# A two-block transformer kernel on one core: the order of the first three weight blocks and of x is changed

## The reference

```python
def rms_norm(x, g):
    y = xf * lax.rsqrt(jnp.mean(xf * xf, axis=-1, keepdims=True) + NORM_EPS)
    return (y * g).astype(x.dtype)
def swiglu(x, w_gate, w_up, w_down):
    return (jax.nn.silu(x @ w_gate) * (x @ w_up)) @ w_down
x = x + 0.5 * swiglu(rms_norm(x, ffn1_norm[l]), ffn1_w_gate[l], ffn1_w_up[l], ffn1_w_down[l])
```

## Time and profile before

| what | value |
|---|---|
| runs, median of 3 | 1061.32 us (1061.10 to 1061.32) |
| span of the profiled execution | 1060.0 us |
| lies around that span, to the median | 1.3 us |
| TensorE busy | 1049.6 us, 99% of the span |
| VectorE, ScalarE, GpSimd busy | 73%, 58%, 18% |
| DMA | 200.53 MB, 189 GB/s over the span |
| chain that ended last | TensorE 97%, ScalarE, VectorE and DMA 1% each |

### The profile page before, as it was taken

One profiled execution on the slowest core, in us unless ns is written; L12 is line 12 of the kernel. 1 busy time (PEld: TensorE's weight loads), 2 busy tenths in 40 slices (PEclk: granted clock), 3 DMA queues, 4 the chain that ended last, 5 costly groups with the idle time before them and its releaser, 6 DMA issues.

```text
span 1060.0 us, 17544 instructions
## 1 busy us (share of the span) xinstructions
PE 1049.6 (99%) x6112; PEld 919.2 (87%) x6112; DVE 772.7 (73%) x1111; ACT 614.9 (58%) x940; POOL 186.7 (18%) x200
## 2 busy tenths in 40 slices
PE   8999999999999999999999999999999999999997
PEld 6888888888888888888888888889988888888885
DVE  6876776799797666668766667787877778767553
ACT  6755545466765664447565445755655566655642
POOL 4211131020221111101111110233201031111100
PEclk9999999999999999999999999999999999999999
DMA  7866565554266655656655564656455556666562
GB/s 268 293 195 196 188 191 182 173 182 161 97 215 202 193 188 185 190 196 201 198 190 189 180 202 154 230 183 190 171 197 181 189 182 202 211 189 194 176 186 76
DMA packets 55714, 200.53 MB, mean 189 GB/s; under 512 B 6320, under 2 KB 6320, under 8 KB 55536
## 3 DMA queue, kind: packets, MB, share of 16 engines
q1 hardware_dynamic: 54288, 195.58, 57.2%
q0 software_dynamic: 656, 3.18, 0.8%
q10 hardware_dynamic: 720, 1.09, 0.4%
HBM read 198.78 MB, written 1.05 MB: 189 GB/s over the span
## 4 chain that ended last, share of the span: by engine, by line
PE 97%; ACT 1%; DVE 1%; DMA 1%; issue 0%; ACTq 0%; DVEq 0%
PE pair L1393 52%; PE pair L1394 26%; PE pair L1387 5%; PE pair L1389 5%; PE pair L1388 5%; DMA x<-x_in 1%; PE pair L1748 0%; PE pair L1681 0%; PE pair L1668 0%; PE pair L1612 0%; PE pair L1659 0%; PE pair L1461 0%; ACT qk_a L682 0%; ACT x_hl L472 0%; DVE qk_a L1175 0%; PE pair L1645 0%
## 5 line engine op out<-in xcount | busy, mean ns | idle before, releaser
L851 DVE TENSOR_TENSOR w_lo<-w_raw,w_hi 128x1024 fp32r<-128x1024 f32 x369 | 460.2, 1252 | 216.7 <-ACT w_hi L465 216.5
L1393 PE MATMUL pair<-x_hl,w_hi 128*128 128x512 f32 x1728 | 591.7, 390 | 1.8 <-DVE x_hl L857 1.6
L465 ACT ACTIVATE w_hi<-w_raw 128x1024 fp32r<-128x1024 f32 x369 | 385.7, 1056 | 232.2 <-PE pair L1394 185.9
L1394 PE MATMUL pair<-x_hl,w_lo 128*128 128x256 f32 x1728 | 477.8, 277 | 0.0
L1393 PEld LDWEIGHTS pair<-x_hl,w_hi 128*128 128x128 f32 x1728 | 324.4, 188 | 71.5 <-DVE w_lo L1370 1.3
L1394 PEld LDWEIGHTS pair<-x_hl,w_lo 128*128 128x128 f32 x1728 | 324.4, 188 | 0.1
L1393 PE MATMUL pair<-wide,w_hi 128*128 128x512 f32 x720 | 247.2, 391 | 0.0
L1394 PE MATMUL pair<-wide,w_lo 128*128 128x256 f32 x720 | 199.6, 277 | 0.0
L1393 PEld LDWEIGHTS pair<-wide,w_hi 128*128 128x128 f32 x720 | 135.2, 188 | 28.9
L378 POOL TENSOR_TENSOR wide<-side,wide 128x256 fp32r<-128x256 f32 x88 | 86.4, 982 | 383.6 <-ACT wide L523 383.6
L1394 PEld LDWEIGHTS pair<-wide,w_lo 128*128 128x128 f32 x720 | 135.1, 188 | 0.0
(11 more groups left out here) (199 smaller groups left out, 859.6 us busy)
## 6 DMA issues: line engine op xcount, KB each, us to landing
w_raw<-stream SPq DMA_DIRECT2D x369, 512.0 KB, 4.3
const<-const_in POOLq DMA_DIRECT2D x1, 1248.0 KB, 9.5
w_raw<-stream SPq DMA_DIRECT2D x4, 256.0 KB, 5.8
rows<-rows_in POOLq DMA_DIRECT2D x1, 576.0 KB, 11.4
x<-x_in ACTq DMA_DIRECT2D x2, 256.0 KB, 5.9
x<-x_in SPq DMA_DIRECT2D x2, 256.0 KB, 7.0
sgu_w<-sgu_w_in POOLq DMA_DIRECT2D x1, 512.0 KB, 14.1
qk_a<-gain_in POOLq DMA_DIRECT2D x1, 512.0 KB, 4.0
```

The lines of the kernel that those rows point to most:

```text
L465: nc.scalar.activation(w_hi[:, slot, at:at + BW], w_raw[:, slot, :], ACT.Copy).then_inc(w_hi_done, 1)
L851: nc.vector.tensor_tensor(w_lo[:, slot, :], w_raw[:, slot, :], w_hi[:, slot, at:at + BW].bitcast(F32), ALU.subtract).then_inc(w_split, 1)
L1393: nc.tensor.matmul(dst, a_hi, b_hl.rearrange("p a s -> p (a s)"), start=first, stop=False, skip_group_check=True)
L1394: return nc.tensor.matmul(dst[:, 0:S], a_lo, b_hl[:, 0, :], start=False, stop=last, skip_group_check=True)
```

## The change

SP's queue now has x chunks 2-3, 4-5 and 6-7 between the halves of blocks 0 and 1, and block 2 in two halves. ScalarE's queue has cols before x 0-1, and no more x 2-3. ScalarE, VectorE and TensorE take the pieces in that order: TensorE does two chunks against block 0, the same two against block 1, and so on. Block 2 is split in halves. No square is taken before both halves of block 2; then come squares 0 and 1, block 3, and squares 2 to 7. The matmul of the sum of squares moves from behind block 3 to behind block 4. One warm-up matmul is dropped. The later feed-forwards keep their order.

```diff
-            for n in range(2):
-                sp.dma_start(w_raw[:, n, 0:HALF], stream[n, :, 0:HALF]).then_inc(half_arrived[n], 16)
...
+            first_half(0)
+            first_half(1)
+            x_pair(1)
+            second_half(0)
+            x_pair(2)
+            second_half(1)
+            x_pair(3)
+            first_half(2)
+            second_half(2)
+            sp.dma_start(w_raw[:, 3, :], stream[3]).then_inc(arrived[3], 16)
...
             def first_input():
...
+                def first_half(n):
+                    act.wait_ge(half_arrived[n], 16)
+                    nc.scalar.activation(w_hi[:, n, 0:HALF], w_raw[:, n, 0:HALF], ACT.Copy).then_inc(half_hi_done, 1)
...
+                first_half(0)
+                act.wait_ge(cols_loaded, 16)
+                x_pair(0)
+                first_half(1)
+                x_pair(1)
+                second_half(0)
+                x_pair(2)
+                second_half(1)
+                x_pair(3)
+                first_half(2)
+                second_half(2)
+                square(0, 0)
+                square(0, 1)
+                split(3)
+                for k in range(2, KC):
                     square(0, k)
...
-                for b in range(3, 8):
+                for b in range(4 if p == 0 else 3, 8):
                     split(n0 + b)
...
+            act.dma_start(cols[:, 0:NCOLS], cols_in).then_inc(cols_loaded, 16)
             act.dma_start(x[:, 0:2, :], x_in[:, 0:2, :]).then_inc(x_loaded[0], 16)
-            act.dma_start(cols[:, 0:NCOLS], cols_in).then_inc(cols_loaded, 16)
-            act.dma_start(x[:, 2:4, :], x_in[:, 2:4, :]).then_inc(x_loaded[1], 16)
...
+                def opening(k, c):
+                    slot, w = (n0 + c) % RING, slice(k * P, (k + 1) * P)
+                    if c == 0:
+                        pe.wait_ge(x_split, 8 * p + k + 1)
+                    last = both(bank[4 + c][:, :], w_hi[:, slot, w], w_lo[:, slot, w], x_hl[:, k, :, :], k == 0, k == KC - 1)
+                    if k == KC - 1:
+                        last.then_inc(w_used, 1)
...
+                    for two in range(0, KC, 2):
+                        for c in range(2):
+                            if two < KC // 2:
+                                pe.wait_ge(half_split, c + 1)
+                            else:
+                                pe.wait_ge(w_split, c + 1)
+                            opening(two, c)
+                            opening(two + 1, c)
+                    pe.wait_ge(half_split, 3)
+                    for k in range(KC):
+                        if k == KC // 2:
+                            pe.wait_ge(w_split, 3)
+                        opening(k, 2)
...
-                sum_squares(p)
+                if p:
+                    sum_squares(p)
...
                     wide_block(n0 + 2 * f, bank[2 * j], x_hl, i, 8)
+                    if p == 0 and f == 2:
+                        sum_squares(p)
                     wide_block(n0 + 2 * f + 1, bank[2 * j + 1], x_hl, i, 8)
...
-WARM = 16
+WARM = 15
```

More of the change, by code:

```diff
@@ L201, in build @@
         arrived = [sem(f"arrived{i}") for i in range(RING)]
-        half_arrived = [sem(f"half_arrived{i}") for i in range(2)]
+        half_arrived = [sem(f"half_arrived{i}") for i in range(3)]
         half_hi_done = sem("half_hi_done")
@@ L1365, in _, with second_half @@
                                         ALU.subtract).then_inc(half_split, 1)
-            for k in range(4):
-                input_lo(0, k)
-            for n in range(2):
+            def second_half(n):
                 dve.wait_ge(w_hi_done, n + 1)
@@ L1371, in _ @@
                                         ALU.subtract).then_inc(w_split, 1)
-            for k in range(4, KC):
-                input_lo(0, k)
-            split(2)
+            first_half(0)
+            input_lo(0, 0)
+            input_lo(0, 1)
+            first_half(1)
+            input_lo(0, 2)
+            input_lo(0, 3)
+            second_half(0)
+            input_lo(0, 4)
+            input_lo(0, 5)
+            second_half(1)
+            input_lo(0, 6)
+            input_lo(0, 7)
+            first_half(2)
+            second_half(2)
             ffn(0, START[0], 0)
@@ L1514, in ffn @@
             def ffn(e, n0, p):
-                if p == 0:
-                    pe.wait_ge(half_split, 2)
-                for k in range(KC):
-                    if k == (KC // 2 if p == 0 else 0):
-                        pe.wait_ge(w_split, n0 + 2)
-                    pe.wait_ge(x_split, 8 * p + k + 1)
-                    w = slice(k * P, (k + 1) * P)
-                    for c in range(2):
-                        slot = (n0 + c) % RING
-                        last = both(bank[4 + c][:, :], w_hi[:, slot, w], w_lo[:, slot, w], x_hl[:, k, :, :], k == 0, k == KC - 1)
-                        if k == KC - 1:
-                            last.then_inc(w_used, 1)
@@ L1528, in ffn @@
-                wide_block(n0 + 2, bank[6], x_hl)
+                def opening(k, c):
[5 more added lines that the diff above has]
+                        last.then_inc(w_used, 1)
+                if p == 0:
+                    for two in range(0, KC, 2):
[11 more added lines that the diff above has]
+                        opening(k, 2)
+                else:
+                    pe.wait_ge(w_split, n0 + 2)
+                    for k in range(KC):
+                        for c in range(2):
+                            opening(k, c)
+                    wide_block(n0 + 2, bank[6], x_hl)
```

16 lines of the change are left out of this document (7 added, 9 removed).

## The result

| kernel | executions | median us | lowest to highest |
|---|---|---|---|
| before | 14 | 1061.22 | 1060.94 to 1061.53 |
| changed | 14 | 1066.08 | 1061.09 to 1066.61 |

The ratio of the changed kernel to the one before is 1.003, 95% interval 1.0022 to 1.0039: slower, where 1059.8 was forecast. The median hides what happened. Five of the fourteen executions took 1061.09 to 1061.36, as the kernel before, and nine 1065.61 to 1066.61. Nothing lies between.

What follows compares the result with a forecast made beforehand. TensorE was taken as the chain from block 2 on. Block 2 1.7 us earlier, less 0.2 to 0.3 for the additions, gave 1.5: span 1058.5, plus 1.3 around it, 1059.8 us; range 1059.2 to 1061.4.

Steps and rivals of the forecast that it cites:

- What bounds the kernel: From block 2 at 15.57 us TensorE is the chain; time won before it is won at the end, barring new waits.
- C: Rival, chance 0.12: GpSimd's additions at 1.54 each end at 24.4, TensorE waits 2.2 behind block 4; 0.4 lost, 1061.7 us.
- D: Rival, chance 0.02: fewer warm-up matmuls and small opening waits leave TensorE at its lower clock level; 1063.6 us.
- Block 2, 1.7 earlier: At the opening: interleaved pieces keep VectorE busy without a gap, so block 2 starts at 13.85 and not 15.57.
- The overhead around the span: Around the profiled span: the runs' median lies 1.3 us above it, so a span of 1058.5 gives 1059.8.
- The squares: Behind block 4: GpSimd's seven additions end at 22.5, so TensorE waits 0.3 us for the sum of squares.
- Net 1.5: At block 5: it starts at 22.95 instead of 24.44, a net gain of 1.5 us.
- Behind it: After block 5: reciprocal at 24.6 against 24.35, 0.4 slack at block 10, later constant loads; costs nothing.

Runs made afterwards that it cites:

- before_reset_mix: The kernel before with one unused float32 matmul with ones in front of the second mixer's gates' loop at 758 us; 1061.58 us.
- before_mix_small: The kernel before with an unused 64-column float32 matmul in each of the four rounds of the gates' loop; 1058.85 us, ratio 0.9978.
- short_sum: The changed kernel with five additions of squares on GpSimd instead of seven, TensorE summing the rest with three matmuls; 1060.65 us, ratio 0.9994.
- warm16: The changed kernel with 16 warm-up matmuls as before; three executions took 1060.99 to 1061.39 us, four 1065.76 to 1066.27.
- sum_at_3: The changed kernel with the matmul of the sum of squares back behind block 3; 1065.56 us.
- squares_alone: The kernel before with only the squares and their sum moved as in the changed one; 1061.39 us (1060.92 to 1066.46).
- wait_behind: short_sum with TensorE waiting behind the sum for two unused GpSimd additions; eight executions took 1060.29 to 1061.51 us, three 1065.49 to 1065.98.

## Why the prediction was wrong

**What bounds the kernel.** Right as far as it went: no wait is listed behind the opening, in any profile. This is the step that failed: that "a microsecond won before block 2 is won at the end, unless a new wait takes it back". It priced a wait at its own length and took one pair of matmuls as a constant of 0.34 to 0.35. The trace of before already had both numbers, 0.35 up to the sum and 0.34 behind it, and I read the difference as the longer first pair of a block. The new wait cost 1.2 where it stood and 4.9 behind it, in nine of fourteen executions. No rival held this: C priced a wait at one microsecond per microsecond, and D looked for a slower clock, which the granted clock doesn't show. That such a wait leads to 0.350 by chance is shown by experiment; why it does is open.

**Block 2, 1.7 earlier.** Its start came at 14.02, forecast 13.85. The first pair came at 6.72 and not 7.55, since half 0a landed 1.4 earlier with the new order of DMAs, where the forecast kept 5.53, and x 0-1 at 5.46, outside the 6.0 to 6.9 given for it. But VectorE was not busy without a gap: x 4-5 landed at 9.6 and not 8.9, and ScalarE waited for it. All behind it on SP's queue landed 0.7 to 0.8 late as well, up to block 3 at 13.5 for 12.7. The term itself was too large for another reason. The profiled execution of before was a late one. The kernels that keep its opening have block 2 at 15.05 and 15.07 (before_reset_mix and before_mix_small), and the changed one at 14.02, so the gain was nearer 1.0. The overhead around the span betrays it: in every execution whose time and span are both known the time is 1.7 to 1.9 above the span, not the 1.3 that I took by setting one execution's span against the median of others; its own time was probably near 1061.8.

**The squares.** The place and the sign were right: TensorE waits for the last addition, block 5 follows. The term was mis-sized: 0.3 forecast, 1.16 measured. The last addition ended at 23.46 and not 22.5. The price of a round, one split and one addition in turn, was right: 1.68 where 1.66 was forecast. (Rival C's flat 1.54 for each of the last six additions would have given 9.2 for the measured 8.49.) What failed was the time at which ScalarE delivers. It ran 0.6 to 0.7 late since x 4-5 and began squares 2 to 7 at 14.49 and not 13.79. So block 3's split started first, at 14.62, and the second addition ended behind it, at 16.44 and not 15.1; the third ended 0.5 late, the three rounds behind it 0.3 and the seventh 0.15 more. The Trainium skill ("SBUF — State Buffer", "SBUF: two separate sides") says that the one that starts first has the port pair for the whole instruction. The trace agrees: the split at 14.62 kept its 1.23 and ended at 15.85, the addition at 14.97 ended 0.59 after it, and from 18.6 on each addition ends 0.6 behind a split and each split 1.1 behind an addition, near the 0.72 and 1.21 that they take alone.

**Net 1.5.** Block 5 starts at 23.86. In kernels with the old opening it is at 23.79 and 23.94 (before_reset_mix and before_mix_small). The net gain at block 5 is nothing, and the lower group at 1061.09 to 1061.36 says the same. It is 1.4 above the forecast of 1059.8: 0.9 from block 5 (23.86 for 22.95) and 0.5 from the overhead (1.8 for 1.3). The other 4.9, in nine of fourteen executions, are the rate. With the wait gone (short_sum) the median was 0.6 lower.

**Behind it.** Right: the reciprocal came at 25.72, later than the 24.6 with the later sum, and no wait for blocks 8 to 10 or the stream followed. **Rival D** fell: with 16 warm-up matmuls the two groups stay (warm16), and the granted clock is full. sum_at_3 shows the clock's price where a wait is long, 0.64 a pair for the 0.59 that D took.

## What to carry to other kernels

Where TensorE is busy without a gap, compare the distance between starts of the same matmul, not busy time: two rates 3% apart looked alike in every summary. A wait of a tenth of a microsecond to one in a stream of matmuls cost up to 4.9 us behind itself here, and by chance, so look at the spread of the times and not only at the median. And set a profile's span against the time of the same execution.

## What the runs showed of the hardware

Two matmuls of fp32r, 512 and 256 columns with a weight load each, follow each other at 0.340 or 0.350 us a pair at the same full granted clock, and keep to one rate for up to hundreds of pairs (487 at 0.350, 507 at 0.340). A wait of TensorE of 0.1 to 1.2 us at the first sum let the slower one in, in 9 of 14, 4 of 12, 4 of 7 and 3 of 11 executions (changed kernel, squares_alone, warm16, wait_behind); without one there, none of 183 executions has the 5 us. A stall of 0.1 near 468 us was followed by it in 4 of 13 profiles. A wait can also end it: the changed kernel's trace has pairs at 0.350 up to 12.3 us and at 0.340 from 12.66 on, behind waits of 0.67 and 0.10. A float32 matmul between two blocks of pairs, with no wait before or behind it, was followed by 0.340 within four pairs in every full-clock profile here. What in TensorE makes the two rates, what decides between them after a wait, and why the same matmul in front of the gates' loop did not help, no run here tells. After 3.8 us without work the granted clock was 0.5 (1.2 GHz) from 24.0 to 27.4 us; after waits of up to 1.2 it stayed full. A 128x1024 subtraction on VectorE and a 128x256 addition on GpSimd, side by side, ended in turn, 1.68 us for one of each.
